# Expert scores of a gated stage as 512 moving columns, with their halves added later, and a new order on ScalarE and VectorE

## The chip, the cores and the metric

The kernel runs on one core of one Trainium2 chip. The time is device microseconds of the execution, taken as the median of several runs of the same program. The profile is of one further execution, whose own time stands beside its span.

## The reference

One layer of a decoder trunk over 256 prompt tokens and 32 sample tokens, 1024 wide: normalised input, one projection, a pooling mixer and sparse attention, an output projection with residual, and then the part that takes most of the time, a product-key retrieval over 128 x 128 single-neuron experts:

```
q = (hf @ w_pq).reshape(N, PEER_HEADS, 2, PEER_HALF)
s = einsum('nhcd,hckd->nhck', q, sub_keys)           # scores against two sets of 128 keys
... top 16 of each half, top 16 of the 256 sums -> eidx (expert), g = softmax(fv)
a = gelu(einsum('td,ted->te', xt, expert_u[et]), approximate=False)
y = einsum('te,ted->td', gt * a, expert_v[et])
```

Each token uses 8 heads x 16 experts, of 16384. All is in float32.

## The kernel before

For the 256 prompt tokens the kernel doesn't gather experts. It computes the products of all tokens with all 16384 rows of expert_u, applies Gelu, multiplies with a weight matrix that is zero where an expert was not chosen, and multiplies the result with all of expert_v. The experts are walked in 128 tiles of 128 rows (a **U tile**, `n`), then 128 tiles of expert_v (a **V row**, `v`). The 32 sample tokens do gather: for each of 32 steps a row of 128 experts is fetched by index, once from expert_u and once from expert_v.

Precision is kept by splitting each float32 operand into a high part and a low part that TensorE takes at its faster float32 format, and adding three products: high x high, high x low, low x high. So each U tile needs `w_hi` and `w_lo` from `w_raw`, and the activations h stand as `h_hi` and `h_lo`, 8 blocks (KC) of 128 x 256 each. `prod_u` (L968) issues for each of 8 blocks three matmuls of 256 moving columns into one bank (2 + s, with s = n mod 4), 24 in all.

Buffers of a U tile form a ring of four. In words, tile n goes like this: SyncE loads `w_raw` (`load_u`, after `prod_done` of tile n - 4); ScalarE rounds it to `w_hi` (`split_w`, L1229, called from `next_w` three tiles ahead); GpSimd subtracts to get `w_lo` (`low_w`, L1489; from tile 116 on VectorE does this, L1826); TensorE multiplies; ScalarE applies Gelu to the bank; the bank is free for tile n + 4 (`act_free`).

The U tiles come in three stages. Tiles 0 to 47 (`ahead`) only put Gelu's result into `store`, while VectorE still finds the top experts. **The gated stage**, tiles 48 to 111, step k = n - 48, also builds the weight matrix, four tokens a step: VectorE writes three 128 x 512 tensors (`hots`, L1788 to L1792: a comparison `eq_ps` in PSUM bank 1, the one-hot `j_hot`, and `i_hot` = comparison x weight), TensorE multiplies j_hot with i_hot (`spread`, L991, four matmuls issued as eight), VectorE moves the result into `store` or multiplies it in (`weigh`, L1810 and L1811), and multiplies the Gelu of the tile before by what is known of the weights (`gate`, L1800). At every odd tile (`DOT_AT` = 49, 51, ...) VectorE also takes a sample step's dot product (`dot`, L1818). It waits for `w_lo_ready` of n + 3, that is for the low half of tile n + 2, for rows that GpSimd fetches (`fetch_u`, L1507, queued between its low halves and waiting for the dot but one before) and for a broadcast row of h that SyncE loads (`load_h`, L530, in one queue with `load_u`, also waiting for an earlier dot). The last stage, tiles 112 to 127, has no spread and no dot; towards its end ScalarE splits the first V rows (`split_v`).

Each engine runs its instructions strictly in the order written. The orders in step k before the change:

- TensorE: prod_u(n), spread(k). The spread waits for `hot_ready` and for the weighing two steps before.
- ScalarE (`gated`): wait for prod_u(n), Gelu(n) in place (columns already weighed in PSUM, the rest into store), split of tile n + 3.
- VectorE: hots(k+1), gate(n-1), dot if n is odd, weigh(k).
- GpSimd: low half of tile n, fetch of a sample step.

A V row (`prod_v`, L1045) is 12 matmuls of 512 moving columns, with `ag_hi` and `ag_lo` (the split of `store[v]`, by ScalarE and by VectorE at L1833) as stationary operand.

## Time and profile before

| | us |
|---|---|
| median of 3 runs | 1050.38 |
| runs | 1049.0, 1050.38, 1057.11 |
| the profiled execution | 1056.62 |
| its span, first to last instruction | 1055.0 |
| mean granted TensorE clock | 0.995 |

From the page: TensorE has 6961 matmuls; VectorE is busy 734.7 us (70% of the span), ScalarE 431.1 (41%), GpSimd 447.9 (42%); DMA moves 225 GB/s on average. Times of instructions are in us from the start of the span; PE is TensorE, PEld its weight loads, ACT ScalarE, DVE VectorE, POOL GpSimd, SP SyncE. A matmul's duration is from its start to the end of its way through the array, so neighbours overlap: the distance between starts is what one costs. In timelines, "x8" is that many merged, and square brackets hold the engine's idle time before the instruction and what ended it.

### The profile page before, as it was taken

What the parts mean: (1) busy time and instruction counts of PE and PEld (TensorE: products, weight loads), DVE (VectorE), ACT (ScalarE), POOL (GpSimd) and SP (SyncE); (2) the same over time, 40 slices, a digit from 0 to 9 for tenths busy, and PEclk for the clock granted to TensorE, in tenths of its full rate; (3) what the DMA queues carried; (4) which work ended last, traced back from release to release, by engine and by line L of the source; (5) the groups of instructions that cost most, each with busy time, mean ns of one, the idle gap of its engine ahead of it and who ended that gap; (6) DMA issues with size and microseconds to landing.
All of it is one profiled execution on the core that took longest, in us unless ns stands there. A gap on an engine that the chain in (4) does not pass through costs nothing.

```text
span 1055.0 us, 19777 instructions
## 1 busy us (share of the span) xinstructions
PE 1033.3 (98%) x6961; PEld 888.2 (84%) x6961; DVE 734.7 (70%) x1486; ACT 431.1 (41%) x747; POOL 447.9 (42%) x329
## 2 busy tenths in 40 slices
PE   6999999999999998999999999999999999999998
PEld 3447778889999998999999999878788887888776
DVE  2549999649999738888888885655455555555554
ACT  2123322343456453343434344544444444444442
POOL 4753333245687876777777771011111111111110
PEclk8999999999999999999999999999999999999999
DMA  9425468358755567888888876676667666676663
GB/s 338 122 88 176 143 207 339 107 201 297 255 181 185 179 231 261 273 281 264 288 278 275 275 236 222 215 267 218 200 227 252 219 226 220 242 243 226 221 219 106
DMA packets 79438, 237.40 MB, mean 225 GB/s; under 512 B 11749, under 2 KB 23661, under 8 KB 78980
## 3 DMA queue, kind: packets, MB, share of 16 engines
q1 hardware_dynamic: 65052, 195.51, 55.1%
q0 software_dynamic: 13040, 40.52, 11.4%
q8 instruction: 37, 0.61, 0.2%
q10 hardware_dynamic: 1280, 0.53, 0.2%
q14 instruction: 29, 0.24, 0.1%
HBM read 233.56 MB, written 3.14 MB: 224 GB/s over the span
## 4 chain that ended last, share of the span: by engine, by line
PE 85%; DVE 9%; DMA 3%; issue 1%; POOL 1%; ACT 1%; ACTq 0%; SPq 0%; DVEq 0%
PE psum L980 33%; PE psum L1045 32%; PE psum L991 5%; PE psum L574 4%; DVE top L1585 3%; DVE work_s L1586 2%; PE psum L810 2%; PE psum L1076 2%; PE psum L783 1%; DMA w_raw<-expert_v 1%; DMA w_raw<-expert_ut 1%; POOL w_lo L1489 1%; PE psum L558 1%; PE psum L590 1%; PE psum L932 1%
## 5 line engine op out<-in xcount | busy, mean ns | idle before, releaser
L1489 POOL TENSOR_TENSOR w_lo<-w_raw,w_hi 128x1024 fp32r<-128x1024 f32 x116 | 281.2, 2429 | 107.4 <-ACT w_hi L1097 106.2
L1097 ACT ACTIVATE w_hi<-w_raw 128x1024 fp32r<-128x1024 f32 x214 | 226.7, 1059 | 211.9 <-PE psum L1045 103.9
L980 PE MATMUL psum<-h_hi,w_hi 128*128 128x256 f32 x1024 | 297.1, 290 | 0.2 <-issue 0.2
L980 PE MATMUL psum<-h_lo,w_hi 128*128 128x256 f32 x1024 | 290.2, 283 | 0.0
L980 PE MATMUL psum<-h_hi,w_lo 128*128 128x256 f32 x1024 | 290.1, 283 | 0.0
L980 PEld LDWEIGHTS psum<-h_hi,w_hi 128*128 128x128 f32 x1024 | 196.8, 192 | 1.9 <-issue 1.6
L980 PEld LDWEIGHTS psum<-h_lo,w_hi 128*128 128x128 f32 x1024 | 197.0, 192 | 0.0
L980 PEld LDWEIGHTS psum<-h_hi,w_lo 128*128 128x128 f32 x1024 | 196.7, 192 | 0.0
L1517 POOL DMA_INDIRECT rows_in<-expert_v,eidx x32 | 44.1, 1379 | 326.3 <-PE psum L1076 321.3
L1826 DVE TENSOR_TENSOR w_lo<-w_raw,w_hi 128x1024 fp32r<-128x1024 f32 x98 | 120.1, 1225 | 77.8 <-ACT w_hi L1097 77.8
L1045 PE MATMUL psum<-w_hi,ag_hi 128*128 128x512 f32 x512 | 160.4, 394 | 2.1 <-DVE ag_lo L1833 2.1
L1045 PE MATMUL psum<-w_hi,ag_lo 128*128 128x512 f32 x512 | 158.1, 390 | 0.0
L1045 PEld LDWEIGHTS psum<-w_hi,ag_hi 128*128 128x128 f32 x512 | 94.2, 188 | 28.9 <-issue 7.2
L1045 PEld LDWEIGHTS psum<-w_hi,ag_lo 128*128 128x128 f32 x512 | 96.1, 188 | 20.5
L1833 DVE TENSOR_TENSOR ag_lo<-store,ag_hi 128x256 fp32r<-128x256 f32 x128 | 54.3, 424 | 71.5 <-PE psum L1045 68.9
L1045 PE MATMUL psum<-w_lo,ag_hi 128*128 128x512 f32 x344 | 92.1, 389 | 0.0
L1045 PEld LDWEIGHTS psum<-w_lo,ag_hi 128*128 128x128 f32 x344 | 64.6, 188 | 13.7
L991 PE MATMUL psum<-i_hot,j_hot 128*128 128x128 f32 x512 | 68.0, 275 | 3.1 <-DVE i_hot L1792 3.1
L1322 ACT ACTIVATE psum<-psum 128x256 f32<-128x256 f32 (+32 forms) x80 | 22.7, 284 | 114.3 <-PE psum L980 114.1
L1826 DVE TENSOR_TENSOR lo_more<-raw_more,w_hi 128x1024 fp32r<-128x1024 f32 x42 | 51.4, 1224 | 24.7 <-ACT w_hi L1097 24.7
L1097 ACT ACTIVATE w_hi<-raw_more 128x1024 fp32r<-128x1024 f32 x42 | 44.4, 1058 | 57.8 <-PE psum L1045 51.7
L991 PEld LDWEIGHTS psum<-i_hot,j_hot 128*128 128x128 f32 x512 | 62.9, 192 | 3.5 <-DVE i_hot L1792 3.5
(286 smaller groups left out, 1383.3 us busy)
## 6 DMA issues: line engine op xcount, KB each, us to landing
w_raw<-expert_ut SPq DMA_DIRECT2D x128, 512.0 KB, 4.9
w_raw<-expert_v SPq DMA_DIRECT2D x86, 512.0 KB, 4.1
raw_more<-expert_v SPq DMA_DIRECT2D x42, 512.0 KB, 4.3
w_slice<-w_pq_cols SPq DMA_DIRECT2D x32, 512.0 KB, 5.4
rows_in<-h_save SPq DMA_DIRECT2D x32, 512.0 KB
w_most<-w_in_blocks SPq DMA_DIRECT2D x8, 699.0 KB, 12.6
w_slice<-w_o_half SPq DMA_DIRECT2D x8, 512.0 KB, 4.7
v_cache<-cache_v POOLq DMA_DIRECT2D x64, 64.0 KB, 3.5
```

The source lines that it names most:

```text
L574: return pe.matmul(psum[:, 4 + (i + 1) % 4, 0:ZQ], hT[:, k, t * P:(t + 1) * P], w_cols(j, k), start=(k == 0), stop=(k == KC - 1))
L810: mm = pe.matmul(psum[:, r % 2, 0:SEQ], w_slice[:, (KC + r) % SLICES, k, :], h2[:, k, 0:SEQ], start=(k == 0), stop=(k == KC - 1))
L980: mm = pe.matmul(psum[:, 2 + s, 0:SEQ], a[:, s, c, :], b[:, c, :], start=(i == 0), stop=(i == 3 * KC - 1))
L991: mm = pe.matmul(psum[:, 6 + s % 2, b * NU:(b + 1) * NU], j_hot[:, s % 2, b, :], i_hot[:, s % 2, b, :], start=True, stop=True, skip_group_ ...
L1045: return pe.matmul(y_bank(i), a[:, t * P:(t + 1) * P], b[:, 4 * h:4 * h + 4, :].rearrange("p c d -> p (c d)"), start=start, stop=stop, ski ...
L1097: return act.activation(out, in_, ACT.Copy)
L1322: a = act.activation(psum[:, 2 + s, 0:done], psum[:, 2 + s, 0:done], ACT.Gelu)
L1489: pool.tensor_tensor(w_lo[:, s], w_raw[:, s], w_hi[:, s].bitcast(F32), ALU.subtract).then_inc(S["w_lo_ready"], 1)
L1517: pool.indirect_dma_start(rows_in[:, u % 2, :], None, v_table, bass.IndirectOffsetOnAxis(ap=eidx[:, u:u + 1], axis=0)).then_inc(row_in[u % ...
L1585: settle(dve.max(best, left))
L1826: dve.tensor_tensor(lo, raw, w_hi[:, s].bitcast(F32), ALU.subtract).then_inc(S["w_lo_dve"], 1)
L1833: dve.tensor_tensor(ag_lo[:, v % 2, :], store[:, v, :], ag_hi[:, v % RING, :].bitcast(F32), ALU.subtract).then_inc(S["ag_lo_ready"], 1)
```

## The change

- h is kept in one tensor `h_split` whose blocks hold the high and then the low part, 2 x 256 columns.
- From tile 48 on, `prod_u` takes `w_hi` once per block with all 512 columns: high x high lands in the first half of the bank, high x low in the second. `w_lo` goes with the high part into the first half. 16 matmuls in place of 24. Tiles 0 to 47 issue the same 24 as before.
- ScalarE copies the second half of the bank to `u_low` in SBUF, and VectorE adds it to the first half (`add_low`) before Gelu.
- ScalarE's order in `gated` becomes: copy, split of n + 3 (or of a V row), wait for the sum, Gelu.
- `i_hot` is no longer VectorE's product but four ScalarE copies of 128 columns with the token's weight as per-partition scale (`hot_i`), one step ahead and in front of `gated`. The spread waits for `j_hot` and `i_hot` apart.
- VectorE's order: hots(k+1) with two tensors, gate(n-1), dot, add_low(n), weigh(k). In the last stage: low half, gate, add_low of the next tile.
- ScalarE's high parts of store 0 and 1 come ahead of the last four tiles, VectorE's low parts of these at tiles 124 and 125, and its low half of V row 3 behind the low part of store 2. The wait for all gates moves from ahead of V row 0 to row 4.

Two hunks that only add `wide=False` to a call are left out below, as are blank lines.

```diff
@@ -285,8 +285,8 @@
     i_hot = take("i_hot", [P, 2, NB, NU])
     H0 = cur[0]
-    h_hi = take("h_hi", [P, KC, SEQ], F32R)
-    h_lo = take("h_lo", [P, KC, SEQ], F32R)
+    h_split = take("h_split", [P, KC, 2, SEQ], F32R)
+    u_low = take("u_low", [P, 2, SEQ])
     cur[0] = H0
...
@@ -966,7 +966,7 @@
                     pe.wait_ge(S["w_lo_dve"], n - LO_FROM + 1)
-            def prod_u(s, n, free=True, late=False):
+            def prod_u(s, n, free=True, late=False, wide=True):
                 pe.wait_ge(S["w_hi_ready"], n + 1)
...
@@ -974,17 +974,22 @@
                 if free:
                     pe.wait_ge(S["act_free"], n - 3)
-                i = 0
+                out = psum[:, 2 + s, 0:SEQ]
                 for c in range(KC):
-                    for a, b in ((w_hi, h_hi), (w_hi, h_lo), (w_lo, h_hi)):
-                        mm = pe.matmul(psum[:, 2 + s, 0:SEQ], a[:, s, c, :], b[:, c, :],
-                                       start=(i == 0), stop=(i == 3 * KC - 1))
-                        i += 1
+                    if wide:
+                        pe.matmul(psum[:, 2 + s, :], w_hi[:, s, c, :], h_split[:, c].rearrange("p a t -> p (a t)"),
+                                  start=(c == 0), stop=False, skip_group_check=True)
+                    else:
+                        for a in range(2):
+                            pe.matmul(out, w_hi[:, s, c, :], h_split[:, c, a], start=(c == 0 and a == 0), stop=False)
+                    mm = pe.matmul(out, w_lo[:, s, c, :], h_split[:, c, 0], start=False, stop=(c == KC - 1),
+                                   skip_group_check=wide)
                 mm.then_inc(S["prod_done"], 1)
             def spread(s, k, free=True):
-                pe.wait_ge(S["hot_ready"], k + 1)
+                pe.wait_ge(S["j_hot_ready"], k + 1)
+                pe.wait_ge(S["i_hot_ready"], k + 1)
                 if free:
...
@@ -996,7 +1001,7 @@
                 if n == 2:
                     pe.wait_ge(S["rs_copied"], 4)
-                prod_u(n % RING, n, n >= RING)
+                prod_u(n % RING, n, n >= RING, wide=False)
                 if n < 12 and n % 3 == 1:
...
@@ -1258,7 +1263,7 @@
             copy_q(1)
             act.wait_ge(S["h2_ready"], KC)
-            copy(h_hi[:], h2[:, :, 0:SEQ]).then_inc(S["h_hi_p"], 1)
+            copy(h_split[:, :, 0, :], h2[:, :, 0:SEQ]).then_inc(S["h_hi_p"], 1)
             copy_q(2)
...
@@ -1316,17 +1321,29 @@
                 next_w(s, m, n, free)
+            def hot_i(k):
+                act.wait_ge(S["eq_ready"], k + 1)
+                if k >= 2:
+                    act.wait_ge(S["g_psum"], k - 1)
+                for b in range(NB):
+                    t = NB * k + b
+                    a = act.activation(i_hot[:, k % 2, b, :], eq_ps[:, b, :], ACT.Copy, scale=wT[:, t:t + 1])
+                a.then_inc(S["i_hot_ready"], 1)
             def gated(m, s, done=SEQ, ends=False):
                 n = RING * m + s
                 act.wait_ge(S["prod_done"], n + 1)
+                copy(u_low[:, s % 2, :], psum[:, 2 + s, SEQ:2 * SEQ]).then_inc(S["u_low_ready"], 1)
+                if ends and s >= 1:
+                    split_v(s - 1)
+                else:
+                    next_w(s, m, n)
+                act.wait_ge(S["u_summed"], n - (G_AT - 1))
                 a = act.activation(psum[:, 2 + s, 0:done], psum[:, 2 + s, 0:done], ACT.Gelu)
                 if done < SEQ:
                     a = act.activation(store[:, n, done:SEQ], psum[:, 2 + s, done:SEQ], ACT.Gelu)
                 a.then_inc(S["act_ready"], 1)
-                if ends and s >= 1:
-                    split_v(s - 1)
-                else:
-                    next_w(s, m, n)
...
@@ -1376,7 +1393,10 @@
                 for s in range(RING):
                     ahead(m, s)
+            hot_i(0)
             for k in range(G_STEPS):
+                if k + 1 < G_STEPS:
+                    hot_i(k + 1)
                 gated((G_AT + k) // RING, k % RING, weighed(k))
...
@@ -1391,14 +1411,15 @@
                      ).then_inc(S["ag_hi_ready"], 1)
+            act.wait_ge(S["g_done"], G_STEPS)
+            for v in range(2):
+                high_ag(v, v, False)
             for s in range(RING):
                 gated(NU // RING - 1, s, ends=True)
-                if s >= 2:
-                    act.wait_ge(S["g_done"], G_STEPS)
-                    high_ag(s - 2, s - 2, False)
-            act.wait_ge(S["act_free"], NU)
             for v in range(NU):
+                if v == RING:
+                    act.wait_ge(S["act_free"], NU)
                 if v + 2 < NU:
...
@@ -1482,7 +1503,8 @@
             pool.wait_ge(S["h_hi_p"], 1)
             pool.wait_ge(S["pnew_ready"], 2)
-            pool.tensor_tensor(h_lo[:], h2[:, :, 0:SEQ], h_hi[:].bitcast(F32), ALU.subtract).then_inc(S["h_lo_p"], 1)
+            pool.tensor_tensor(h_split[:, :, 1, :], h2[:, :, 0:SEQ], h_split[:, :, 0, :].bitcast(F32),
+                               ALU.subtract).then_inc(S["h_lo_p"], 1)
...
@@ -1782,15 +1804,20 @@
                 token = slice(NB * k, NB * (k + 1))
                 if k:
-                    dve.wait_ge(S["hot_ready"], k)
+                    dve.wait_ge(S["i_hot_ready"], k)
+                dve.tensor_tensor(eq_ps, bc(iota_ps, 1, NB), bc(iT[:, token], 2, NU), ALU.is_equal
+                                  ).then_inc(S["eq_ready"], 1)
                 if k >= 2:
                     dve.wait_ge(S["g_psum"], k - 1)
-                dve.tensor_tensor(eq_ps, bc(iota_ps, 1, NB), bc(iT[:, token], 2, NU), ALU.is_equal
-                                  ).then_inc(S["eq_ready"], 1)
-                dve.tensor_tensor(j_hot[:, k % 2], bc(iota_ps, 1, NB), bc(jT[:, token], 2, P), ALU.is_equal)
-                dve.wait_ge(S["eq_ready"], k + 1)
-                dve.tensor_tensor(i_hot[:, k % 2], eq_ps, bc(wT[:, token], 2, NU), ALU.mult
-                                  ).then_inc(S["hot_ready"], 1)
+                dve.tensor_tensor(j_hot[:, k % 2], bc(iota_ps, 1, NB), bc(jT[:, token], 2, P), ALU.is_equal
+                                  ).then_inc(S["j_hot_ready"], 1)
+            def add_low(n):
+                s = n % RING
+                dve.wait_ge(S["u_low_ready"], n - (G_AT - 1))
+                dve.tensor_tensor(psum[:, 2 + s, 0:SEQ], psum[:, 2 + s, 0:SEQ], u_low[:, s % 2, :], ALU.add
+                                  ).then_inc(S["u_summed"], 1)
...
@@ -1842,16 +1869,20 @@
                 if n in DOT_AT:
                     dot(DOT_AT.index(n))
+                add_low(n)
                 weigh(k)
             for n in range(G_END - 1, NU):
-                gate(n % RING, n, G_STEPS)
-                if n >= NU - 2:
-                    low_ag(n - (NU - 2), False)
                 if n + 3 >= LO_FROM:
                     low_w(n + 3)
-            low_w(NU + 3)
+                gate(n % RING, n, G_STEPS)
+                if n + 1 < NU:
+                    add_low(n + 1)
+                if n in (NU - 4, NU - 3):
+                    low_ag(n - (NU - 4), False)
             for v in range(2, NU):
                 low_ag(v)
+                if v == 2:
+                    low_w(NU + 3)
                 if v + 2 < NU:
```

## Rows read from the trace of the kernel before

**Rows 1.** page part 1, first line: busy us (share of the span) xinstructions.
```profile
PE 1033.3 (98%) x6961; PEld 888.2 (84%) x6961; DVE 734.7 (70%) x1486; ACT 431.1 (41%) x747; POOL 447.9 (42%) x329
```

**Rows 2.** busy by stretch: length, each engine, granted TensorE clock, DMA share, GB/s.
```profile
381.00:628.50 247.50, 244.39 (x2061) 243.99 (x2061) 208.86 (x437) 96.96 (x194) 188.17 (x97) 0.99 0.82 273
```

**Rows 3.** chain of waits, gated stage and last tiles: start us, us, what.
```profile
421.60 2.87 PE psum L980 x24
587.33 2.87 PE psum L980 x24
628.77 46.26 PE psum L980 x384
```

**Rows 4.** timeline of TensorE, one V row: start us, us, what.
```profile
808.93 0.62 PE L1045 MATMUL psum<-w_hi,ag_hi 128*128 128x512 f32 x2
811.65 0.62 PE L1045 MATMUL psum<-w_hi,ag_hi 128*128 128x512 f32 x2
```

**Rows 5.** timeline of VectorE, GpSimd and ScalarE around one dot product.
```profile
536.66 2.40 POOL L1489 TENSOR_TENSOR w_lo<-w_raw,w_hi 128x1024 fp32r<-128x1024 f32 x1
539.09 1.22 DVE L1818 SCALAR_TENSOR_TENSOR rows_in<-rows_in 128x1024 f32<-128x1024 f32 x1 [1.60 <-POOL w_lo L1489]
539.31 1.06 ACT L1097 ACTIVATE w_hi<-w_raw 128x1024 fp32r<-128x1024 f32 x1 [1.36 <-DMA w_raw<-expert_ut]
540.24 0.32 DVE L1810 COPY store<-psum 128x164 f32<-128x164 f32 x1
540.45 2.39 POOL L1489 TENSOR_TENSOR w_lo<-w_raw,w_hi 128x1024 fp32r<-128x1024 f32 x1 [1.39 <-ACT w_hi L1097]
540.91 0.69 DVE L1788 TENSOR_TENSOR psum<-psum,iT 128x512 f32<-128x512 f32 x1
```

**Rows 6.** timeline of VectorE (gate, then weighing) and ScalarE (Gelu, then split).
```profile
610.29 0.39 DVE L1800 TENSOR_TENSOR store<-psum,store 128x232 f32<-128x232 f32 x1
610.60 0.23 DVE L1810 COPY store<-psum 128x88 f32<-128x88 f32 x1
631.68 0.37 ACT L1322 ACTIVATE psum<-psum 128x256 f32<-128x256 f32 x1 [1.34 <-PE psum L980]
631.96 1.05 ACT L1097 ACTIVATE w_hi<-w_raw 128x1024 fp32r<-128x1024 f32 x1
```

**Rows 7.** timeline of ScalarE, and its groups by shape (count, busy us, mean ns).
```profile
107.37 0.37 ACT L1185 ACTIVATE prob_p<-psum,small 128x128 f32<-128x128 f32 x1
107.63 0.19 ACT L1185 ACTIVATION_READ_ACCUMULATOR prob_p<-psum,small 128x1 f32 x1
371.84 0.27 ACT L1097 ACTIVATE jT<-psum 128x128 f32<-128x128 f32 x1
372.00 0.28 ACT L1097 ACTIVATE wT<-psum 128x128 f32<-128x128 f32 x1
...
L1207 ACT ACTIVATE catT<-psum,gains 128x288 f32<-128x288 f32 x4 | 2.0, 501 | 0.3 <-PE psum L763 0.3
L1097 ACT ACTIVATE dT<-psum 128x288 f32<-128x288 f32 x4 | 1.6, 411 | 7.8 <-PE psum L721 7.8
```

**Rows 8.** an early dot, GpSimd beside it, TensorE's waits on i_hot, the clock after.
```profile
389.60 4.73 POOL L1489 TENSOR_TENSOR w_lo<-w_raw,w_hi 128x1024 fp32r<-128x1024 f32 x2
392.04 3.38 DVE L1818 SCALAR_TENSOR_TENSOR rows_in<-rows_in 128x1024 f32<-128x1024 f32 x1 [3.07 <-POOL w_lo L1489]
...
PE psum L991 <- DVE i_hot L1792: 3.1, 2, 1.9
...
416.00:418.50 2.50, 2.50 (x14) 2.50 (x14) 2.50 (x5) 0.28 (x1) 0.25 (x1) 0.50 1.00 388
```

**Rows 9.** timeline of ScalarE and TensorE at the first spread.
```profile
384.92 1.06 ACT L1097 ACTIVATE w_hi<-w_raw 128x1024 fp32r<-128x1024 f32 x1 [1.95 <-DMA w_raw<-expert_ut]
385.26 1.06 PE L991 MATMUL psum<-i_hot,j_hot 128*128 128x128 f32 x8
```

**Rows 10.** waits of TensorE: us in total, times, longest us.
```profile
PE psum L1045 <- DVE ag_lo L1833: 2.1, 3, 0.9
```

More of the change, by code:

```diff
@@ L1009, in _ @@
                 for s in range(RING):
-                    prod_u(s, RING * m + s)
+                    prod_u(s, RING * m + s, wide=False)
             for t in range(3):
@@ L1020, in _ @@
                 for s in range(RING):
-                    prod_u(s, RING * m + s)
+                    prod_u(s, RING * m + s, wide=False)
             pe.wait_ge(S["slots_copied"], 3)
```

## The prediction

> **What bounds the kernel now.** Page part 1 first: TensorE is busy 98% of the span [rows 1], so a wait counts only where it reaches TensorE. The table by stretch narrows that to the gated stage (tiles 48 to 111), which in 247.5 us has 3.1 us of TensorE idle, with VectorE busy 209 us, GpSimd 188 us and ScalarE only 97 us [rows 2]. The chain of waits shows its beat: 24 matmuls take 2.87 us; from the tile that starts at 421.60 to the one at 587.33 there are 44 steps, so 3.767 us each, with no break [rows 3]. The rest, 0.90 us, is the spread with its change-over. The last 16 tiles run 384 matmuls in 46.26 us. So TensorE sets the beat, and the question is what the other engines can hold once it is shorter.
>
> **Matmuls.** Per contraction block, three matmuls of 256 columns at 2.87/24 = 0.1196 us become one of 512 and one of 256. A V row, 12 matmuls of 512, takes 808.93 to 811.65, or 0.2267 us each [rows 4]. A block goes from 0.3587 to 0.3463, a tile gains 8 x 0.0124 = 0.10 us. 64 gated tiles: **-6.4 us**; 16 last tiles: **-1.6 us**. Bounds: nothing, if the mixed widths lose the fixed part again; -8 otherwise. I take it whole, as the operands have the shapes of rows 3 and 4. A pair of gated tiles then wants 7.34 us instead of 7.54.
>
> **VectorE and ScalarE by load.** VectorE loses one 512-wide product (0.60 us) and gains a sum of 256 (0.33 us): a 232-wide product releases the next instruction after 0.31 [rows 6]. ScalarE gains a copy of 256 (0.28 us, as Gelu of 256 before the split at 631.96 [rows 6]) and four scaled copies of 128. Neither is full. By load alone nothing is lost, but the order of waits is another matter.
>
> **The ring of waits.** Every odd tile n has a dot product on VectorE that waits for GpSimd's low half of tile n+2. In the steady state this low half runs 536.66 to 539.06, the dot starts at 539.09, weighing starts at 540.24, the next comparison at 540.91 [rows 5]. Today ScalarE never waits for any of this. In the new order it does: Gelu(n) waits for the sum, which stands behind dot(n) on VectorE; behind that Gelu stand hot_i, the copy for n+1 and the split of n+4; that split feeds GpSimd's low half, which dot(n+2) waits for. Once round: dot 1.15, sum 0.33, weighing 0.67, comparison 0.69 and 0.03 to ScalarE, four hot_i spacings 4s, copy 0.28, split 1.06 and 0.08 to GpSimd, low half 2.40, 0.03 back = 6.72 + 4s per two tiles [rows 5, 6]. The Gelu itself hides beside weighing and comparison. GpSimd's fetch (about 1 us after a dot) hides beside the ScalarE part.
>
> **What s is.** Plain 128-wide copies out of PSUM follow each other every 0.16 us and last 0.27. One with a per-partition operand lasts 0.37, and the same difference shows at 288 wide: 501 against 411 ns. What follows it starts after 0.26 [rows 7]. No two such instructions stand back to back here unpaced, so: lower bound s = 0.16 (operand fetch hidden), upper 0.37 (no overlap). I take 0.26, since the overlap of 0.11 is seen on both kinds. The ring is then 7.76 us against 7.34: 0.42 more per pair, also above today's 7.54.
>
> The Trainium skill (ScalarE: Activation LUTs, What ACT_TABLE_LOAD costs) says that each per-partition pointer operand adds about 93 ns to an activation and that neighbours overlap by as much. Rows 7 agree on the first (90 to 100 ns). By the page's own formula s would be 0.29, the ring 7.90, and the forecast some 4 us higher.
>
> It binds when hot_i is late for its spread: from a dot's start to the end of the next odd hot_i there are 1.15 + 0.33 + 0.67 + 0.72 + 1.14 = 4.0 us, so a dot may start at most 7.34 - 4.0 = 3.3 us after its tile's end. Now it starts some 1.6 after (the next tile starts at 421.60 + 31 x 3.767 = 538.37, the end before the spread is 0.9 earlier). That slack of 1.7 us is gone after four pairs; the other 28 pay 0.42: **+11.8 us**. A late dot also holds SyncE (the broadcast load of h waits for it, and the U loads stand behind), which adds landings that come later but have the same beat.
>
> **What the old stalls do.** Early in the stage the trace has two waits of the spread for i_hot, 3.1 us in all, and after the longer, 1.9, TensorE's granted clock is 0.50 (1.2 GHz) for 2.5 us and more [rows 8]. From the first spread at 385.26 to tile 57 at 421.60 there are one spread and 8 steps, 0.9 + 8 x 3.767 = 31.0 us by the beat; they took 36.3, so with the clock's part and 0.2 us for where the chain lets a tile begin, the stalls cost 5.1 [rows 3, 9]. Their cause is a dot that lasts 3.38 us because GpSimd began the next low half just before it: the pair 389.60 to 394.33 runs unbroken, and the dot ends a microsecond after it [rows 8]. The new order spaces the splits by hot_i, so this doesn't recur there: **-5.1 us** against the profiled run. The median run is 6.2 us below the profiled one, about these stalls, so I take it not to have them.
>
> **Start of the stage.** The first spread now needs ScalarE's hot_i(0), which stands behind the split that ran 384.92 to 385.98 after a late landing. It ends at 387.0, and the spread moves from 385.26 by **+1.75 us** [rows 9]. Bounds 0 (landing early) and 2.5.
>
> **Handing over to the last 16 tiles.** At tile 111 there is no further hot_i, so ScalarE splits 114 at once and GpSimd begins its low half right behind that of 113, just ahead of dot(111). The dot is blocked as in rows 8: 3.3 us until VectorE goes on. Then sum and hop 0.45, Gelu and the small one after it 0.45, copy 0.28, split 1.06, 0.08, low half 2.40 = 8.0 us after low half 113. TensorE wants tile 115 at three tiles plus spread, 9.0 us, after the end of 111, and the ring is 3.3 to 4 us late by then. Stall: **+2.6 us** (0 if the dot is not blocked). The Trainium skill (SBUF — State Buffer, Who interferes with whom) states this as an exclusive lock between a VectorE instruction with two SBUF inputs and a GpSimd one that reads SBUF; rows 8 agree, and by it the sum of a PSUM and an SBUF operand is not touched.
>
> **Clock.** The wait of 1.9 us halved it for 2.5 us and somewhat more, of which half is lost, 1.3 to 1.7; the other, of 1.2 us, did not [rows 8]. Two stalls of that order are new (1.75 and 2.6); I count one dip: **+1.6**, bounds 0 and 3.4.
>
> **V rows.** TensorE waited 2.1 us in three places for ag_lo [rows 10]. The splits of store 0 and 1 come ahead of the last Gelus and ag_lo(2) ahead of a low half, so two of the three go; the landings of V weights stay: **-1.2**, bounds 0 and -2.1. The last Gelus and gates come later, behind splits, but nothing needs them before the fourth V row. **At no cost:** the new layout of h (one copy and one subtraction of the same size, behind the last scores' matmuls), the 48 tiles before (same matmuls, same order), one more semaphore on the spread. If the cover fails, that is under 1 us each.
>
> **Sum** against the profiled execution (1056.62, span 1055.0): -6.4 - 1.6 + 11.8 - 5.1 + 1.75 + 2.6 + 1.6 - 1.2 = +3.5, so 1060.1. Against the median 1050.4, without the -5.1: 1059.0. I say **1059 us**.
>
> **Rivals.**
> A, not slower: the pointer operand hides behind the copy before, s = 0.16. The ring is 7.36, a tie with TensorE. Terms: -6.4 - 1.6 - 5.1 + 1.4 - 1.2, a few pairs late 0.6, half a hand-over stall and clock 2.1 = -10.2, so 1046 to 1047. For it: 0.16 is what plain ones do. Against: the extra 0.09 is in each duration. It decides at s = 0.205, where the ring equals the old 7.54.
> B, much slower: no overlap, s = 0.37, ring 8.20, 31 pairs x 0.86 = 26.7 instead of 11.8: 1074. For it: the 288-wide scaled copies are 0.49 apart; but TensorE paced these.
> C: the blocked dot recurs within the stage, 2.2 us a time. By the ring, split(n+3) ends 0.7 us after dot(n) starts, a thin margin; ten times is +22: 1081.
> D: the late sum never matters since landings set ScalarE's times anyway (it waited for them up to 4.9 us early on), and the wide matmuls give their 8 us: 1041. Against: in the steady state those waits are 0 to 2 us, and the ring doesn't contain them.
>
> **How the numbers follow.** Forecast 0.60, A 0.22, B 0.08, C 0.05, D 0.05. A difference of 1% (10.5 us) is what I treat as told from no change: 1039.9 to 1060.9. The forecast's own width is about 1055 to 1063 by start, hand-over and clock, so a third of it is over the bound: slower 0.20 + 0.13 + 0.02 = 0.35; faster only from the edge of D, 0.04; same 0.61. The range takes in A and leaves out C, most of B and D: 1045 to 1067.
>
> **What would show it.** Right: even steps of about 3.67 and odd of about 4.1 us in the gated stage; the spread waiting for ScalarE's hot_i; dots 3.5 to 4 us after their tile's end; scaled copies 0.26 apart; one dot of over 3 us at the end and a stall before tile 115. A V row, and the first 382 us, unchanged. Wrong: copies 0.16 apart, dots that stay under 2 us behind, or 512-wide matmuls in the U tiles that take more than 0.23 us.

## The result and the profile after

The changed kernel takes **1059.09 us**, median of 19 runs (1055.88 to 1063.06), against 1051.81 us for the kernel before, 19 runs on the same chips (1049.0 to 1057.78). The ratio is 1.0065 with a 95% interval of 1.0048 to 1.0081: 7 us or 0.65% slower, which the interval tells from no change. The forecast was 1059, "same" by its bound of 1%. The profiled execution is the fastest of the 19: 1055.88 us, span 1054.2, 3.2 below the median; the last part of this section says what the traces show of those 3.2 us.

Part 1 of the page, beside [rows 1]:

```profile
PE 1028.3 (98%) x6321; PEld 850.8 (81%) x6321; DVE 721.2 (68%) x1502; ACT 516.5 (49%) x1083; POOL 456.5 (43%) x329
```

The 640 matmuls less are there. TensorE's busy time falls by only 5.0 us and its share stays at 98%, so this part doesn't show what happened. The chain of engines in part 4 does, first before, then after the change:

```profile
PE 85%; DVE 9%; DMA 3%; issue 1%; POOL 1%; ACT 1%; ACTq 0%; SPq 0%; DVEq 0%
```
```profile
PE 65%; DVE 17%; POOL 7%; ACT 7%; issue 2%; DMA 1%; ACTq 0%; DVEq 0%
```

A fifth of the span has gone from TensorE to a chain over the other engines. The chain of waits (start us, us, what) says which: where [rows 3] had one tile of TensorE behind another, there is now GpSimd's low half and the dot product.

```profile
411.04 2.41 POOL w_lo L1511
413.48 1.23 DVE rows_in L1845 x2
418.79 2.42 POOL w_lo L1511
...
628.05 2.41 POOL w_lo L1511
630.49 3.41 DVE rows_in L1845 x2
```

From 411.04 to 628.05 there are 28 rounds, 7.750 us each. The timeline of one round (start us, us, engine, line, operation, and in brackets the idle time before it and what ended it), beside [rows 5]:

```profile
514.26 1.22 DVE L1845 SCALAR_TENSOR_TENSOR rows_in<-rows_in 128x1024 f32<-128x1024 f32 x1 [0.95 <-POOL w_lo L1511]
...
515.41 0.43 DVE L1819 TENSOR_TENSOR psum<-psum,u_low 128x256 f32<-128x256 f32 x1
515.75 0.34 DVE L1837 COPY store<-psum 128x188 f32<-128x188 f32 x1
515.87 0.27 ACT L1343 ACTIVATE psum<-psum 128x136 f32<-128x136 f32 x1 [0.95 <-DVE psum L1819]
...
516.41 0.69 DVE L1808 TENSOR_TENSOR psum<-psum,iT 128x512 f32<-128x512 f32 x1
...
517.13 1.14 ACT L1331 ACTIVATE i_hot<-psum,wT 128x128 f32<-128x128 f32 x4 [0.81 <-DVE psum L1808]
...
518.15 0.40 ACT L1102 ACTIVATE u_low<-psum 128x256 f32<-128x256 f32 x1
...
518.41 1.08 ACT L1102 ACTIVATE w_hi<-w_raw 128x1024 fp32r<-128x1024 f32 x1
...
519.57 2.41 POOL L1511 TENSOR_TENSOR w_lo<-w_raw,w_hi 128x1024 fp32r<-128x1024 f32 x1 [0.72 <-ACT w_hi L1102]
```

Start to start: dot 1.15, sum 0.34, weighing 0.66, comparison to hot_i 0.72, four hot_i 1.02, copy 0.26, split 1.16, low half 2.44 to the next dot: 7.75. Such a closed round of waits over several engines is called a ring here. TensorE keeps 3.67 to 3.75 us from one spread to the next in its first eleven steps; then it waits for this ring, in a pattern of four tiles (4.10, 3.81, 3.81, 3.79) that adds up to two rounds. The whole stage, 63 steps from one spread to the next, takes 242.08 us; before they were 242.45, of which 5.1 were the early stalls [rows 8].

At the end of the stage, timeline of all engines:

```profile
628.05 4.75 POOL L1511 TENSOR_TENSOR w_lo<-w_raw,w_hi 128x1024 fp32r<-128x1024 f32 x2 [1.81 <-ACT w_hi L1102]
630.49 3.40 DVE L1845 SCALAR_TENSOR_TENSOR rows_in<-rows_in 128x1024 f32<-128x1024 f32 x1 [1.70 <-POOL w_lo L1511]
...
634.28 0.37 ACT L1343 ACTIVATE psum<-psum 128x256 f32<-128x256 f32 x1 [4.72 <-DVE psum L1819]
...
636.08 2.35 POOL L1511 TENSOR_TENSOR w_lo<-w_raw,w_hi 128x1024 fp32r<-128x1024 f32 x1 [3.28 <-ACT w_hi L1102]
638.53 0.47 PE L980 MATMUL psum<-h_split,w_hi 128*128 128x512 f32 x1 [2.09 <-issue]
648.61 1.06 ACT L1102 ACTIVATE w_hi<-w_raw 128x1024 fp32r<-128x1024 f32 x1 [3.87 <-DMA w_raw<-expert_ut]
651.03 0.47 PE L980 MATMUL psum<-h_split,w_hi 128*128 128x512 f32 x1 [1.16 <-issue]
```

The blocked last dot and the stall before tile 115 are there. The stall of 1.16 us behind tile 118 was not forecast. The load for tile 119 was issued at 641.58, when the late tile 115 was done and its buffer free, and it took 7.0 us to land; the median of the eight loads of that stretch is 4.1.

**The first spread**, beside [rows 9]. Of the profiles in this document, eight build `i_hot` on ScalarE and so start this stage as the change has it. The first line is the change's; under it are the three of the eight with the longest waits:

```profile
384.78 1.13 PE L996 MATMUL psum<-i_hot,j_hot 128*128 128x128 f32 x8 [1.00 <-ACT i_hot L1331]
```
```profile
386.60 1.50 PE L996 MATMUL psum<-i_hot,j_hot 128*128 128x128 f32 x8 [2.01 <-ACT i_hot L1331]
```
```profile
386.88 1.13 PE L996 MATMUL psum<-i_hot,j_hot 128*128 128x128 f32 x8 [2.22 <-ACT i_hot L1331]
```
```profile
387.31 1.86 PE L996 MATMUL psum<-i_hot,j_hot 128*128 128x128 f32 x8 [2.29 <-ACT i_hot L1331]
```

The three are narrow matmuls, an earlier dot, and Gelu first at the hand-over (experiments 4, 6 and 7). ScalarE's hot_i(0) stands behind a split whose load lands late. In these three the first step after the wait took 5.3 us instead of 3.7 or 3.8, as the granted clock fell to 0.50, the 1.2 GHz level. In the other four of the eight (experiments 1, 2, 8 and 9) the waits are 0.89, 1.47, 1.53 and 0.85 us, and no such fall follows. The table by stretch shows it for the last of the three, and the start of the run (length, busy time of TensorE, its weight loads, VectorE, ScalarE, GpSimd, granted clock, DMA share, GB/s); under it the start of the run in the change's profile, which has no such stretch at all:

```profile
16.00:20.00 4.00, 4.00 (x13) 0.98 (x13) 1.14 (x3) 0.00 (x0) 1.82 (x4) 0.64 1.02 391
388.00:390.00 2.00, 2.00 (x9) 1.84 (x9) 1.10 (x3) 2.00 (x6) 1.52 (x2) 0.50 0.66 268
```
```profile
16.00:20.00 4.00, 4.00 (x16) 1.22 (x14) 1.62 (x4) 0.00 (x0) 1.83 (x4) 1.00 1.02 380
```

A run like these three has, against the profiled run of the change, 0.8 to 1.2 us more ahead of the wait, 1.0 to 1.3 by the longer wait and 1.6 by the clock behind it: 3.4 to 4.1 together, where the median is 3.2 above. But other ways lead there too: experiments 1, 2 and 9 have no fall of the clock at the first spread and still reach the end of this wait 2.6 to 5.3 us later than the change's profile, as their runs were later before it. The mean granted clock says a little. In the profiles a run whose one fall of 3.4 us is at the start has a mean of 0.998 (experiments 11 and 12); 10 of the 19 runs are below that, so a second fall is likely in about half of them. Where the other runs lose their time is not shown.

### The profile page after: what moved, and what is told of

Read it like the earlier page. It is cut to its first block, busy times and chain, and to the rows that moved or that the text cites. A ratio compares the mean times of both kernels' runs of the same rounds, so it can differ in the third digit from the quotient of the medians.

```text
span 1054.2 us, 18894 instructions
## 1 busy us (share of the span) xinstructions
PE 1028.3 (98%) x6321; PEld 850.8 (81%) x6321; DVE 721.2 (68%) x1502; ACT 516.5 (49%) x1083; POOL 456.5 (43%) x329
## 4 chain that ended last, share of the span: by engine, by line
PE 65%; DVE 17%; POOL 7%; ACT 7%; issue 2%; DMA 1%; ACTq 0%; DVEq 0%
PE psum L1050 33%; PE psum L984 9%; POOL w_lo L1511 7%; PE psum L985 5%; PE psum L574 4%; DVE rows_in L1845 4%; ACT w_hi L1102 3%; ACT i_hot L1331 3%; DVE top L1607 3%; DVE work_s L1608 2%; PE psum L980 2%; DVE psum L1808 2%; PE psum L810 2%; PE psum L1081 2%; PE psum L783 1%
## 5 line engine op out<-in xcount | busy, mean ns | idle before, releaser
L1511 POOL TENSOR_TENSOR w_lo<-w_raw,w_hi 128x1024 fp32r<-128x1024 f32 x116 | 288.5, 2492 | 108.1 <-ACT w_hi L1102 107.8
L985 PE MATMUL psum<-h_split,w_lo 128*128 128x256 f32 x1024 | 287.1, 280 | 0.0
L980 PE MATMUL psum<-h_split,w_hi 128*128 128x512 f32 x640 | 231.8, 403 | 3.3 <-issue 3.3
L985 PEld LDWEIGHTS psum<-h_split,w_lo 128*128 128x128 f32 x1024 | 194.4, 190 | 0.0
L980 PEld LDWEIGHTS psum<-h_split,w_hi 128*128 128x128 f32 x640 | 120.3, 188 | 29.1 <-ACT w_hi L1102 2.4
L984 PE MATMUL psum<-h_split,w_hi 128*128 128x256 f32 x768 | 140.3, 285 | 1.0 <-issue 0.5
L984 PEld LDWEIGHTS psum<-h_split,w_hi 128*128 128x128 f32 x768 | 119.5, 192 | 2.7 <-issue 1.9
L1331 ACT ACTIVATE i_hot<-psum,wT 128x128 f32<-128x128 f32 x256 | 73.0, 368 | 40.0 <-DVE psum L1808 40.0
L1102 ACT ACTIVATE w_hi<-raw_more 128x1024 fp32r<-128x1024 f32 x42 | 44.5, 1059 | 57.8 <-PE psum L1050 50.2
```

The lines of the kernel that those rows point to most:

```text
L980: pe.matmul(psum[:, 2 + s, :], w_hi[:, s, c, :], h_split[:, c].rearrange("p a t -> p (a t)"), start=(c == 0), stop=False, skip_group_check ...
L984: pe.matmul(out, w_hi[:, s, c, :], h_split[:, c, a], start=(c == 0 and a == 0), stop=False)
L985: mm = pe.matmul(out, w_lo[:, s, c, :], h_split[:, c, 0], start=False, stop=(c == KC - 1), skip_group_check=wide)
L1102: return act.activation(out, in_, ACT.Copy)
L1331: a = act.activation(i_hot[:, k % 2, b, :], eq_ps[:, b, :], ACT.Copy, scale=wT[:, t:t + 1])
L1511: pool.tensor_tensor(w_lo[:, s], w_raw[:, s], w_hi[:, s].bitcast(F32), ALU.subtract).then_inc(S["w_lo_ready"], 1)
```

## The experiments

Each is one edit of the changed kernel, or several of these edits together, with 6 to 12 runs, against the kernel before on the same chip (its medians there 1051.6 to 1053.1). The step is the time from one spread to the next.

**1. The dot behind the sum.** On VectorE the ring's first link is cut: ScalarE's Gelu no longer waits for the dot.

```diff
-                if n in DOT_AT:
-                    dot(DOT_AT.index(n))
                 add_low(n)
                 weigh(k)
+                if n in DOT_AT:
+                    dot(DOT_AT.index(n))
```

> VectorE's dot product moves behind sum and weighing of its own step; nothing else differs from the changed kernel. Theory (ring of waits): the ring loses sum and weighing, 7.76 - 0.33 - 0.67 = 6.76 us per two tiles, under TensorE's 7.34, so the gated stage falls to about 3.67 us a tile and the kernel to 1059 - 32 x 0.41 = 1046, up to 1050 if some dots are now blocked by GpSimd (over 3 us long). Rival 1 (ScalarE simply has too much to do in this stage, or the landings are late): its work is the same, so 1057 to 1060. Rival 2 (the dots collide with GpSimd more often when they come later): most dots last over 3 us and the kernel is over 1060.

Measured: 1053.25 us (1047.40 to 1056.67), ratio 0.9998 (0.9973 to 1.0022), profiled 1050.34. The 63 steps took 234.35 us, 7.7 less than in the change. The ring was what paced the stage. But the time is 3 us above the 1050 that the theory allowed at most, and the ring isn't all: TensorE keeps 3.67 to 3.72 us for half of the stage, and then the pattern 3.84, 3.82, 3.67, 3.67 comes, 7.50 us for two tiles. The timeline there:

```profile
592.86 0.69 DVE L1808 TENSOR_TENSOR psum<-psum,iT 128x512 f32<-128x512 f32 x1
...
593.59 1.14 ACT L1331 ACTIVATE i_hot<-psum,wT 128x128 f32<-128x128 f32 x4 [0.45 <-DVE psum L1808]
...
594.60 0.40 ACT L1102 ACTIVATE u_low<-psum 128x256 f32<-128x256 f32 x1
...
595.03 0.43 DVE L1819 TENSOR_TENSOR psum<-psum,u_low 128x256 f32<-128x256 f32 x1 [0.60 <-ACT u_low L1102]
595.38 0.25 DVE L1837 COPY store<-psum 128x100 f32<-128x100 f32 x1
...
596.04 1.22 DVE L1845 SCALAR_TENSOR_TENSOR rows_in<-rows_in 128x1024 f32<-128x1024 f32 x1
...
597.18 0.69 DVE L1808 TENSOR_TENSOR psum<-psum,iT 128x512 f32<-128x512 f32 x1
```

A second ring, without GpSimd: comparison, hot_i, copy, sum, weighing, (dot), next comparison, 4.32 us with a dot and 3.18 without, 7.50 a pair. VectorE waits for ScalarE and ScalarE for VectorE once per tile. The same orders are in the change, where the first ring of 7.75 us is the longer one; the prediction did not see the second. In this run TensorE also waits 1.82 us for ag_hi at the first V rows, which it does not in the change's. The runs spread over 9 us, and the slower half isn't explained by the one profile.

**2. hot_i with a constant scale** (the gate weights are left out of the sum).

```diff
-  ... ACT.Copy, scale=wT[:, t:t + 1])
+  ... ACT.Copy, scale=1.0)
```

> hot_i's four copies take a constant scale of 1.0 in place of the token's weight, so the weights of the prompt tokens are left out of the result. Theory: the spacing s falls from 0.26 to 0.16 and the ring from 7.76 to 7.36 us per two tiles, a tie with TensorE; 1047 to 1049. Rival (the per-partition operand costs nothing where it matters, the pace comes from elsewhere): 1057 to 1060, with the same 7.75 us.

Measured: 1047.84 us (1045.75 to 1050.74), ratio 0.9958 (0.9936 to 0.9980), steps 232.19 us in all, each 3.67 to 3.75. As the ring says: the copies now start 0.163 us apart, so it is 7.38. The groups of ScalarE by shape (count, busy us, mean ns, idle before), of this kernel and of the change:

```profile
L1331 ACT ACTIVATE i_hot<-psum 128x128 f32<-128x128 f32 x256 | 50.3, 283 | 39.3 <-DVE psum L1808 39.3
```
```profile
L1331 ACT ACTIVATE i_hot<-psum,wT 128x128 f32<-128x128 f32 x256 | 73.0, 368 | 40.0 <-DVE psum L1808 40.0
```

The per-partition operand costs 85 ns in duration and 92 ns in spacing. Four of them a tile cost 11.3 us of kernel time (1059.1 against 1047.8), of which 9.9 are in the steps, since they stand in the ring.

**3. i_hot on VectorE again.** The change's other parts stay.

```diff
-            hot_i(0)
             for k in range(G_STEPS):
-                if k + 1 < G_STEPS:
-                    hot_i(k + 1)
...
+                dve.wait_ge(S["eq_ready"], k + 1)
+                dve.tensor_tensor(i_hot[:, k % 2], eq_ps, bc(wT[:, token], 2, NU), ALU.mult
+                                  ).then_inc(S["i_hot_ready"], 1)
```

> i_hot is VectorE's product again, as before the change; wide matmuls, sum and ScalarE's new order stay. Theory: the ring is dot 1.15, sum 0.45, Gelu 0.36, copy 0.28, split 1.06, low half 2.4 and hops 0.2 = 5.9 us and no longer binds; VectorE's own work is 3 x 0.60 + 0.30 + 0.33 + 0.67 a tile and half a dot of 1.15, 7.4 us per two tiles, so it binds just above TensorE's 7.34: 1048 to 1051. Rival (moving i_hot to ScalarE is what lets the stage keep up, VectorE being full): 1062 or more.

Measured: 1045.24 us (1043.26 to 1050.07), ratio 0.9920 (0.9890 to 0.9949): faster than before and than expected. VectorE is busy 233 us of 248 in this stage and still keeps 3.67 to 3.72 us a tile, so the expected limit of 7.4 us a pair by VectorE's load was not there. The slowest run was the profiled one; three dots in it are blocked as in [rows 8]:

```profile
442.92 4.73 POOL L1508 TENSOR_TENSOR w_lo<-w_raw,w_hi 128x1024 fp32r<-128x1024 f32 x2
...
445.35 3.39 DVE L1845 SCALAR_TENSOR_TENSOR rows_in<-rows_in 128x1024 f32<-128x1024 f32 x1 [1.13 <-POOL w_lo L1508]
...
451.78 1.15 PE L996 MATMUL psum<-i_hot,j_hot 128*128 128x128 f32 x8 [1.06 <-DVE i_hot L1812]
```

Each makes a step of 4.9 to 6.3 us. So spacing the splits by hot_i, as the change does, had indeed removed these stalls; without it they come back, now and then.

**4. Narrow matmuls in the change**, 24 of 256 columns a tile (the copied half is the first one times zero, as there is no second).

```diff
-            def prod_u(s, n, free=True, late=False, wide=True):
+            def prod_u(s, n, free=True, late=False, wide=False):
...
-                copy(u_low[:, s % 2, :], psum[:, 2 + s, SEQ:2 * SEQ])...
+                act.activation(u_low[:, s % 2, :], psum[:, 2 + s, 0:SEQ], ACT.Copy, scale=0.0)...
```

> All U tiles use the 24 matmuls of 256 columns again; everything else of the change stays (ScalarE's copy to u_low reads the first half times 0, so the sum adds zeros). Theory (the ring paces the gated stage at 7.75 us per two tiles, above the 7.54 of narrow matmuls): the stage takes the same time, the last 16 tiles lose 1.6 us less what their stalls give back; 1059 to 1061. Rival (TensorE's beat plus something per tile sets the pace): 80 x 0.10 us more, 1067.

Measured: 1060.03 us (1058.09 to 1063.00), ratio 1.0067 (1.0041 to 1.0093), steps 242.76, of which 1.6 are the clock behind the first spread. That is 0.9 us above the change, and 0.2 by the ratios, which the intervals don't tell from nothing. TensorE keeps its own 3.77 until step 28 here, but for the first, and then comes the same pair of 7.75: the wide matmuls, 8 us of TensorE's work, give almost nothing there, because the ring and not TensorE sets the beat.

**5. Narrow matmuls without the ring:** the edits of 3 and 4 together.

> i_hot on VectorE, and all U tiles with 24 matmuls of 256 columns, as before the change; the copy, the sum and the orders of the change stay (the copied half is the first one times zero, since there is no second). Theory: with the ring gone TensorE paces this stage, so the narrow matmuls cost the full 80 x 0.10 = 8 us: 1052 to 1054 us against 1045.2 with wide ones, steps of 3.77 us. Rival: wide matmuls give nothing at the start of the stage and at the stalls, and the stalls are fewer with the slower beat: 1047 to 1050 us.

Measured: 1053.85 us (1048.33 to 1058.60), ratio 1.0003 (0.9978 to 1.0029), steps 3.76 and 3.77 but for two behind blocked dots. Against 3 (0.9920) that is 0.83%, 8.7 us: here the wide matmuls give what they should. The intervals of the two, taken as independent, leave 5 to 13.

**6. What holds the dot.** GpSimd's low half and the dot follow each other in the ring. Either the semaphore wait alone orders them, or the dot can't go on beside a running low half at all. Here the dot waits for the low half before the one it waits for now.

```diff
-                dve.wait_ge(S["w_lo_ready"], DOT_AT[u] + 3)
+                dve.wait_ge(S["w_lo_ready"], DOT_AT[u] + 2)
```

> The changed kernel, but the dot product of tile n waits for GpSimd's low half of tile n+1 instead of n+2. Theory 1, the link from GpSimd's low half to the dot product is the order written out by this wait: the dot starts earlier in the gated stage, the ring opens, steps are 3.67 to 3.75 us and the time is 1046 to 1051 us. Theory 2, the link is the one that rows 8 show, a dot product beside a running low half doesn't go on: dots then last 2 to 3.5 us and end about a microsecond after the low half as now, two steps still take 7.6 to 7.8 us and the time is 1056 to 1060 us.

Measured: 1050.59 us (1047.69 to 1055.08), ratio 0.9980 (0.9959 to 1.0000). The time is that of theory 1, the trace that of theory 2:

```profile
512.74 2.41 POOL L1511 TENSOR_TENSOR w_lo<-w_raw,w_hi 128x1024 fp32r<-128x1024 f32 x1 [0.73 <-ACT w_hi L1102]
...
514.15 2.08 DVE L1845 SCALAR_TENSOR_TENSOR rows_in<-rows_in 128x1024 f32<-128x1024 f32 x1
...
516.16 0.42 DVE L1819 TENSOR_TENSOR psum<-psum,u_low 128x256 f32<-128x256 f32 x1
```

The dot starts at 514.15 beside a low half that runs until 515.15, and what follows it starts 1.01 us after that end. Waiting at the semaphore, in the change, it was 0.03 + 1.15 = 1.18 us behind the end. So a dot issued into a running low half does not finish before that ends, but saves 0.17 us, and the dots are 7.59 us apart instead of 7.75. Both theories had a part wrong: the ring stays, and 0.17 us of 7.75 a pair is worth more than expected, as only the part above TensorE's 7.37 counts. The ring is 0.22 above it instead of 0.38, over 22 pairs instead of 26: 4.8 us instead of 9.9 (TensorE first waits for it after some 20 steps). Most of the rest of the 8.5 us between this kernel and the change is at the hand-over: the last dot takes 2.8 us instead of 3.4 and starts 1.9 us behind the last spread instead of 3.6, and neither of the two stalls behind it, 2.09 and 1.16 us in the change, is in this trace; TensorE's longest wait in the last 16 tiles is 0.28.

The Trainium skill (SBUF — State Buffer, Who interferes with whom) has it that a VectorE instruction with two SBUF inputs and a GpSimd one that reads SBUF contend, and that whoever issues first gets the shared pair of ports "for the whole instruction". The traces agree: the dot here, issued 1.00 us before the low half ends, takes 2.08 us instead of 1.22, and it takes 3.39 where GpSimd's next low half begins just ahead of it (experiment 3).

**7. Gelu before the split in tile 111**, so that the low half of 114 can't begin before the last dot.

```diff
-                else:
+                elif not hold:
                     next_w(s, m, n)
                 act.wait_ge(S["u_summed"], n - (G_AT - 1))
                 ...
                 a.then_inc(S["act_ready"], 1)
+                if hold:
+                    next_w(s, m, n)
...
-                gated((G_AT + k) // RING, k % RING, weighed(k))
+                gated((G_AT + k) // RING, k % RING, weighed(k), hold=(k == G_STEPS - 1))
```

> The changed kernel, but in tile 111 alone ScalarE takes Gelu before the split of tile 114, so that GpSimd can't begin the low half of 114 until the dot product of 111 is done. Theory: that low half, begun 0.03 us before the dot, is what made the last dot 3.4 us, and so the stall of 2.1 us before tile 115 and the one of 1.2 us after tile 118. Expected: last dot 1.2 us, both stalls gone or halved, 1055.5 to 1057.5 us against 1059.1. Rival: the split of 114 moved behind the sum comes as late by itself as the blocked dot made things: dot short, stall before tile 115 still 1.5 to 2.5 us, 1058 to 1060 us.

Measured: 1057.91 us (1056.19 to 1063.12), ratio 1.0059 (1.0038 to 1.0081), which isn't told from the change's 1.0065. No dot over 1.3 us, and the stall before tile 115 stays:

```profile
633.79 1.23 DVE L1847 SCALAR_TENSOR_TENSOR rows_in<-rows_in 128x1024 f32<-128x1024 f32 x1 [1.71 <-POOL w_lo L1513]
...
635.41 0.37 ACT L1343 ACTIVATE psum<-psum 128x256 f32<-128x256 f32 x1 [3.50 <-DVE psum L1821]
...
639.27 0.47 PE L980 MATMUL psum<-h_split,w_hi 128*128 128x512 f32 x1 [2.39 <-issue]
```

The rival's way: the split, now late itself, takes the place of the blocked dot.

**8. Sum and weighing before the dot in tile 111 alone.**

```diff
-                if n in DOT_AT:
+                if n in DOT_AT and n != G_END - 1:
                     dot(DOT_AT.index(n))
                 add_low(n)
                 weigh(k)
+                if n == G_END - 1:
+                    dot(DOT_AT.index(n))
```

> The changed kernel, but in tile 111 alone VectorE takes the sum and the weighing ahead of the dot product. Theory: the hand-over stall comes from Gelu of tile 111, and so the copy of 112 and the split of 115, standing behind that dot product; with the sum first, the split of 115 starts some 4 us earlier, both stalls of TensorE (2.1 us before tile 115, 1.2 us after tile 118) go, and the dot product may last 3.4 us without harm: 1055 to 1056.5 us against 1059.1. Rival: TensorE is released from the ring 3 us late in any case and the stalls are set by the loads of tiles 115 and 119, so one of 1 to 2 us remains: 1057 to 1059 us.

Measured: 1057.69 us (1053.79 to 1061.12), ratio 1.0046 (1.0026 to 1.0067). That is inside the rival's range, with one stall of the size that it gave, but for a reason that neither names:

```profile
630.47 3.40 DVE L1845 SCALAR_TENSOR_TENSOR rows_in<-rows_in 128x1024 f32<-128x1024 f32 x1 [0.72 <-POOL w_lo L1511]
...
633.92 0.23 ACT L1402 ACTIVATE a_s<-dots 128x32 f32<-128x32 f32 x1 [4.12 <-DVE rows_in L1845]
634.08 0.39 ACT L1102 ACTIVATE u_low<-psum 128x256 f32<-128x256 f32 x1
...
637.95 0.47 PE L980 MATMUL psum<-h_split,w_hi 128*128 128x512 f32 x1 [1.62 <-issue]
```

ScalarE has a Gelu over all dot products directly behind the gated stage. It waits for the last dot, and the copy of 112 and the split of 115 stand behind it.

**9. The edit of 8, and that Gelu behind tile 123.**

```diff
-            act.wait_ge(S["dots_done"], NS)
-            act.activation(a_s[:, :], dots[:, :], ACT.Gelu).then_inc(S["a_s_ready"], 1)
             with act.Fori(G_END // RING, NU // RING - 1) as m:
                 for s in range(RING):
                     gated(m, s)
+            act.wait_ge(S["dots_done"], NS)
+            act.activation(a_s[:, :], dots[:, :], ACT.Gelu).then_inc(S["a_s_ready"], 1)
```

> The changed kernel with, in tile 111, the sum and the weighing ahead of the dot product, and with ScalarE's Gelu over all dot products moved behind tile 123. With the first of the two alone, ScalarE still stood 4.1 us at that Gelu, which waits for the last dot product, and the copy of 112 and the split of 115 stood behind it: TensorE had a stall of 1.6 us. Theory: there were two links from the last dot to the split of 115, and with both gone the stalls of 2.1 us before tile 115 and 1.2 us after tile 118 go: 1054.5 to 1056.5 us against 1059.1, most dips of the clock in this stretch with them. Rival: the loads of 115 and 119 are the limit, stall of 1 to 2 us stays, 1057 to 1058.5 us.

Measured: 1055.62 us (1051.81 to 1060.25), ratio 1.0034 (1.0014 to 1.0053). The last dot still takes 3.40 us and no wait of TensorE is left in the last 16 tiles. The two stalls together are 3.25 us in the change, 1.62 in experiment 8 and nothing here; the medians go from 1059.09 over 1057.69 to 1055.62, 3.5 us in all, and 3.3 by the ratios. The intervals tell the whole of it from nothing, but neither half by itself; the halves rest on the traces.

**10. i_hot on VectorE and the dot last** (edits 3 and 1), **11. with edit 7 as well**, **12. with edit 9's Gelu instead.**

> i_hot is built on VectorE again and VectorE takes the dot product after the sum and the weighing. In the run with i_hot on VectorE alone (1045.24 us, profiled 1050.07) TensorE's steps were 3.67 to 3.72 us except around three blocked dot products of 3.4 us, each with a step of 4.9 to 6.3 us. Theory: what is left are these blocked dots, and they cost because sum and weighing stand behind them; with the dot last, a blocked one delays only the next comparison, which has some 2 us of slack. Expected 1041 to 1044 us, no step over 4.5 us. Rival: the comparison behind the dot is what the spread needs next, so nothing is saved, or the dot comes later and is blocked more often: 1045 to 1050 us.

> i_hot on VectorE, the dot product after sum and weighing, and in tile 111 Gelu before the split of 114: all three repairs on the changed kernel. Theory: TensorE paces the whole gated stage at 3.67 to 3.72 us a tile and the hand-over has no stall: 1040 to 1043 us, which is the 8 us of the wide matmuls plus what the V rows give, below the kernel before. Rival: the hand-over repair only moves the split late and adds a stall of 1 to 2 us where there was none: 1 to 2 us above the same kernel without it.

> i_hot on VectorE, the dot product always after sum and weighing, and the Gelu over all dot products behind tile 123; the split of 114 stays where the change has it. Theory: neither ring nor hand-over stall is left, only one or two blocked dots early in the stage, when loads land late: 1041.5 to 1043.5 us, with little spread from run to run. Rival: splitting 114 early costs more through the blocked dot than the moved Gelu gives: 1044 to 1048 us, as in the run without the moved Gelu (1047.0).

Measured: 10: 1047.04 us (1043.42 to 1051.01), ratio 0.9937 (0.9911 to 0.9963). 11: **1043.40 us** (1042.23 to 1045.64), ratio 0.9912 (0.9881 to 0.9942). 12: 1044.83 us (1043.38 to 1045.98), ratio 0.9923 (0.9899 to 0.9947). Ten is 3 above what was expected: the rival's figure. In its trace the last dot takes 3.33 us and two early dots are blocked, with steps of 4.73 and 5.69, so the dot behind sum and weighing does not take the sting out of a blocked one: the next comparison is what TensorE waits for. Eleven is 0.4 above what was expected, and twelve, expected at 1041.5 to 1043.5, lies in its rival's range of 1044 to 1048; its last dot again takes 3.33 us. All three, and experiment 3, are faster than both kernels. Their intervals overlap, so which of them is best is not shown. The chain of waits of 11 in the gated stage is TensorE again, as in [rows 3]:

```profile
582.20 0.89 PE psum L996 x8
585.88 0.89 PE psum L996 x8
```

## Why the prediction was right, step by step

**Matmuls, -6.4 and -1.6.** About right in size, and absent where it was booked. Experiments 3 and 5 give 8.7 us for 8.0, with 5 to 13 left open; their steps give 7.0, as a step falls from 3.767 to 3.685 (5.2 us in 64) and one of the last tiles from 2.88 to 2.77 (1.8 in 16). A block of the tile has the forecast 0.346 us. In the change itself (against 4) they are worth 0.9 at most by the medians, not told from nothing. The sum had it right, because the ring was priced against the shorter beat of 7.34; but the sentence "a tile gains 0.10 us" is not what a reader would find in the trace. The step came out 0.02 us longer than -0.10 makes it (3.685, not 3.669, so 7.37 a pair): the spread's change-over did not stay what it was.

**The ring, 6.72 + 4s with s = 0.26.** Right: 7.75 measured for 7.76, four hot_i take 1.02 us to the copy behind them, s = 0.255. The rivals A (0.16) and B (0.37) turned on this one spacing, and experiment 2 is rival A made real: 1047.8 for the 1046 to 1047 that A gave. Of the signs, the dots start 3.5 to 3.6 us behind their tile, as forecast, and the spread waits for hot_i. The steps are not 3.67 and 4.1 in turn, but 4.10, 3.81, 3.81 and 3.79; why the pair of 7.75 is shared out so is not shown.

The Trainium skill (ScalarE: Activation LUTs, What ACT_TABLE_LOAD costs) gives about 93 ns for a pointer operand; experiment 2 shows 85 in duration. By its formula s was to be 0.29, an estimate from its figures; the trace has 0.255, and the measurement decides.

**+11.8 for it.** Mis-sized by 2: 242.08 us against 232.19 in experiment 2 are 9.9. The slack lasted eleven steps, not eight, and each pair then paid 0.38 over 7.37, not 0.42 over 7.34: 26 x 0.38 = 9.9.

**Old stalls, -5.1.** Right for the profiled run; the change's profile has no blocked dot before the last, and experiment 3's, without hot_i between the splits, has three. That a median run of the kernel before has none of these stalls is taken for granted in the sum; the one profile of that kernel can't show it.

**Start, +1.75.** 0.85 to 2.29 in eight profiles. **Clock, +1.6.** Seen in three of these eight, at the first spread, where the wait was 2.01 us or more; the 2.09 us before tile 115 in the change was not followed by a stretch at 1.2 GHz, and the change's own profile has no such stretch until its end. Experiment 7's 2.39 us before tile 115 was. How many of the 19 runs pay the term is open.

**Hand-over, +2.6.** The stall was there (2.09, and 1.16 more behind tile 118; 3.5 us by experiments 8 and 9). The named cause was only one of several: the blocked dot need not be there (7), and the sum behind the dot is one of two links (8); the Gelu over the dots, which is in the code in plain sight, is the other. The step came out near because both end at the same dot: the low half of 115 ends 8.0 us behind that of 113, as added up.

**V rows, -1.2.** 378.12 us from the first V row to the end instead of 379.17, and one wait of 0.6 us for ag_lo instead of three with 2.1 [rows 10].

**The profiled run** should have been 1060.1 by the sum and was 1055.88. Of these 4.2 us, 1.9 are the ring's size, 1.6 the fall of the clock that this run lacks, 0.75 its short first wait and 1.5 the stretch ahead of that wait, which this run, at full clock from the start, has shorter than the run before. Against that stand 1.2 for the smaller gain of the gated steps and 0.6 for the second hand-over stall; 0.2 to 0.3 are left over.

That the median came out at 1059.09 for 1059.0 is partly luck. The forecast was 8.6 us above the median before, and the measured difference is 7.3; but the median before was taken from three runs, 1050.38, and is 1051.81 in nineteen. The two errors cancel. Within the sum the ring is 2 too dear, the matmuls give 1 less than booked by the steps, and the hand-over is booked 1 too low.

**Not seen:** the second ring of 7.50 us (experiment 1). It would have decided the case had the dot been last. Nor that TensorE's speed at the start of a run differs from one profile to the next.

## What to carry to other kernels

When work moves from a loaded engine to an idle one, busy time says nothing: write down every round of waits that the new order closes, add up one round of each from start-to-start times in the trace, and compare each with the beat of the engine that bounds; here two rounds of 7.75 and 7.50 us stood against 7.37, and undoing the move of i_hot turned a loss of 7 us into a gain of 7 to 9 (experiments 3, 10, 11 and 12). In such a round a spacing of 0.09 us more in four small instructions cost 10 to 11 us, and 8 us saved on TensorE gave nothing that the runs could tell. When a stall is traced to one late instruction, look for every instruction queued behind something that waits for it: with one of two links removed a stall of 1.6 us was left, with both none, and the kernel was 3.5 us faster.

## What the runs showed of the hardware

- Four ScalarE copies 128 columns wide out of PSUM with a per-partition scale last 368 ns and stand 255 ns apart; with a constant scale they last 283 ns and stand 163 ns apart.
- A VectorE instruction with two SBUF inputs, issued 1.0 us before the end of GpSimd's subtraction, let the next one start 0.17 us sooner after that end than one that waited for it at a semaphore (1.01 against 1.18 us). In this ring, starting it into the collision was cheaper than waiting.
- GpSimd is held the same way: in experiment 1 a low half that was issued 0.04 us behind the dot of 596.04 took 3.42 us instead of 2.41:

```profile
596.08 3.42 POOL L1511 TENSOR_TENSOR w_lo<-w_raw,w_hi 128x1024 fp32r<-128x1024 f32 x1 [0.54 <-ACT w_hi L1102]
```

- VectorE was busy 233 us of 248 and TensorE behind it still kept its beat of 3.685 us:

```profile
382.00:630.00 248.00, 242.79 (x1564) 218.71 (x1563) 233.20 (x508) 118.18 (x260) 196.57 (x98) 0.99 0.81 274
```

(Experiment 3; the 5.2 us in which TensorE is idle are mostly its waits behind the blocked dots.)

- In the gated stage and at its end, waits of TensorE of 2.01, 2.22, 2.29, 2.39 and 2.43 us (the last in experiment 3) were followed by 3.4 us at 1.2 GHz, and in the kernel before one of 1.9 by a like stretch [rows 8]. After waits of 1.81, 1.86, 1.94 and 2.09 us the granted clock stayed at 1.00 (experiments 2, 10 and 4, and the change), and it did after one of 2.32 in experiment 5, here with the stretch behind it:

```profile
415.62 1.13 PE L996 MATMUL psum<-i_hot,j_hot 128*128 128x128 f32 x8 [2.32 <-DVE i_hot L1812]
416.00:419.00 3.00, 3.00 (x28) 3.00 (x27) 3.00 (x7) 1.15 (x4) 1.21 (x1) 1.00 0.99 374
```

So the length of the wait alone does not decide it.
